# Eleven convolution taps go from TensorE to ScalarE products and GpSimd sums; VectorE's nine are all done in the projection

## The chip, the cores and the metric

The kernel runs on one core of one Trainium2 chip. The metric is the device time of one execution in microseconds, as the median of several runs. One execution was profiled; its trace and its page are what the numbers below are read from. PE is TensorE, DVE is VectorE, ACT is ScalarE, POOL is GpSimd, SP is SyncE, which here issues nearly all transfers.

## The reference

One step of a decoder layer for a prompt of 512 tokens and for 8 sample tokens. The part that matters here is the mixing sub-layer:

```python
z = rms_norm(x, norm_g) @ w_in                      # 1024 -> 2048 columns
gm_u, gm_v, cv_a, cv_b = jnp.split(z, [...], axis=-1)   # 512 each
u = jax.nn.gelu(gm_u)
v = layer_norm(jax.nn.gelu(gm_v), gm_ln_g, gm_ln_b)     # over each head's 128 channels
a_out = u * chunk_spatial_mix(v, gm_ws, gm_bs)
glu = cv_a * jax.nn.sigmoid(cv_b)
full = jnp.concatenate([conv_past, glu], axis=1)
conv = depthwise_conv(full, conv_w)  + conv_b           # 31 taps per channel, causal
b_out = jax.nn.silu(layer_norm(conv, cv_ln_g, cv_ln_b))
y = x + jnp.concatenate([a_out, b_out], axis=-1) @ w_out
```

After it come keys and values of 256 memory tokens, cross-attention with 4 heads, a mixture of 32 experts (one group of four, then two of its eight experts for each token) and a final norm. All is float32.

## The kernel before

Each engine has its own instruction list, and semaphores order the engines against each other. Nothing is scheduled by a tool: the order in the code is the order on the engine. Every engine waits in place, so what stands behind a waiting instruction waits too.

**Projection.** The product with w_in has 16 column blocks of 128 channels, m = 0 to 15, with the tokens along the free axis. Each float32 product is made of three passes (a high part and a low part of weights and activations, lines 1708 to 1710), 48 matmuls a block. For this ACT writes the high part w_h of a pair of blocks (split_h, line 739) and DVE the low part w_l (split_l, line 1057), one pair ahead. DVE takes each block out of PSUM and multiplies it by the token's norm rstd (line 1182). Blocks 0, 1, 4, 5 become the linear half of glu; blocks 2, 3, 6, 7 are its gates (ACT's sigmoid, then a DVE product that counts the semaphore glu_ready up); blocks 8 to 11 are v, and 12 to 15 are u (both by ACT's gelu, line 788). The norms rstd come out of a small chain: DVE writes five diagonal tiles, PE turns them into a row with all-ones matmuls (token_norms, line 1746), DVE copies the row (line 1118) and can only then empty the first blocks. token_norms stands behind block 2, and block 3 of PE needs the first block's PSUM back.

**Convolution.** glu has 4 groups of 128 channels, with 30 zero columns in front. A tap is a shifted copy of glu times one weight per channel. Of the 31 taps DVE does the first nine (V_TAPS) as `conv = glu * w + conv` (part_taps, lines 1148 and 1151), 36 instructions of 128x512: 28 of them between the blocks of the projection, by the table PART_AT, eight later. PE does the other 22 after the projection (conv_taps): per tap 16 matmuls of 32x512 with diagonal weights dw, each recorded as two, so 32 records a tap at line 1829. In front of the last tap PE adds DVE's part with one more group of 16 (line 1824), for which it waits for part_done. Between the taps stand four turnings of the memory tokens (mem_turned), which ACT and DVE empty.

**Around it.** After the projection DVE normalises v, 128 channels of 128 tokens at a time (line 1222), and POOL scales and shifts each tile by ln_g and ln_b (lines 2216 and 2218). PE needs v only behind the first block of memory keys. PE's next stage, the memory keys, follows the convolution directly; ACT empties the convolution's PSUM (line 820).

POOL does one mask and nothing else between its first 2 us and the normalisation of v. SP loads weight slots in one fixed order (STREAM); slots come free as split_l reads them.

Of the kernel before, what the change touches and what calls it, by code (L numbers as in the profile page):

```python
# [22 lines left out]
F32 = mybir.dt.float32  # L23
F32R = mybir.dt.float32r
I32 = mybir.dt.int32
ALU = mybir.AluOpType
# [3 lines left out]
P = 128  # L30
D = 1024
KT_D = D // P
SEQ = 512
NS = 8
# [9 lines left out]
PE_TAPS = TAPS - V_TAPS  # L44
# [117 lines left out]
def trunk_kernel(nc, a, outs):  # L162
# [6 lines left out]
    with ExitStack() as ctx:  # L169
# [93 lines left out]
        tail = at("tail", [PAST + NS, GM], F32, kT_at)  # L263
# [17 lines left out]
        mem_junk = at("mem_junk", [P, D], F32, kT_at + 4096)  # L281
# [130 lines left out]
        part_done = sem("part_done")  # L412
        conv_out = sem("conv_out")
# [7 lines left out]
        v_ready = sem("v_ready")  # L421
        v_scaled = sem("v_scaled")
# [4 lines left out]
        tail_stored = sem("tail_stored")  # L427
        gmv_stored = sem("gmv_stored")
# [18 lines left out]
        r_root = sem("r_root")  # L447
        x_stored = sem("x_stored")
        gk_in = sem("gk_in")
# [87 lines left out]
        def _(sp):  # L537
# [48 lines left out]
            for c in range(AT[("w_in", 1)], len(STREAM)):  # L586
# [12 lines left out]
                if c == 16:  # L599
                    sp.wait_ge(ta_used, TA_AT["tail"] + 1)  # L600
                    sp.dma_start(conv_prompt[0, 0], tail[0:PAST, :]).then_inc(tail_stored, 16)
                    sp.dma_start(conv_sample[0, :, PAST - 1, :], tail[PAST:PAST + NS, :]).then_inc(tail_stored, 16)
                if c == 16:
                    sp.wait_ge(v_ready, NT)
                    sp.dma_start(gmv_prompt[0, 0], v_tok[:, 3, :]).then_inc(gmv_stored, 16)
                    sp.dma_start(gmv_sample[0, :, 0, :], v_s[0:NS, :]).then_inc(gmv_stored, 16)
# [106 lines left out]
            sp.wait_ge(tail_stored, 32)  # L713
            sp.wait_ge(gmv_stored, 32)
# [6 lines left out]
        def _(act):  # L721
# [53 lines left out]

            for n in range(8):
# [51 lines left out]
            for n in range(8, 16):  # L828
                split_h(n + 1)
                if n == 9:  # L830
# [4 lines left out]
                    act.wait_ge(gmv_stored, 32)  # L835
# [114 lines left out]
            act.dma_start(gk[:], a["norm_ffn_g"][0].rearrange("(p k) -> p k", k=KT_D)).then_inc(gk_in, 16)  # L950
# [18 lines left out]
            act.activation(rs5[:], rs5[:], ACT.Sqrt).then_inc(r_root, 1)  # L969
# [34 lines left out]
            act.wait_ge(gk_in, 16)  # L1004
# [29 lines left out]
        def _(dve):  # L1034
# [86 lines left out]
            def tap_weights(i):  # L1121
# [5 lines left out]
                w = cols_b[:, V_TAPS:TAPS, i:i + 1].broadcast_to([P, PE_TAPS, BAND])  # L1127
# [36 lines left out]
            PART_AT = {4: 3, 5: 4, 6: 4, 7: 3, 8: 2, 9: 3, 10: 3, 11: 3, 14: 3}  # L1164
# [39 lines left out]
            dve.tensor_scalar(mv[:, :, :, 1], mv[:, :, :, 1], EPS, None, ALU.add).then_inc(v_mean, 1)  # L1204
            part_taps(2)
# [1162 lines left out]
```

## Time and profile before

| | |
|---|---|
| median of three runs | 686.86 us (686.58 to 687.76) |
| the profiled execution | 687.92 us, its span 686.0 us |
| TensorE busy | 595.5 us (87% of the span) |
| VectorE busy | 318.0 us (46%) |
| ScalarE busy | 197.9 us (29%) |
| GpSimd busy | 78.8 us (11%) |
| mean granted TensorE clock | 0.939 |
| HBM | 174.94 MB read, 15.61 MB written |

The span runs from the first to the last instruction; 1.9 us of the execution's own time lie around it. Shares of the span are averages over stages with different limits: the projection runs to 108.6 us, the convolution to 138.2, memory keys, output projection and attention to about 347, routing to 420, and the experts to 650.

### The profile page before, as it was taken

The page shows a single profiled execution, that of the slowest core. Times are in us where ns is not written, and L with a number is a line of the kernel's source. Part 1 is how long each engine was busy: PE and PEld are TensorE (multiplying, and loading weights), DVE is VectorE, ACT ScalarE, POOL GpSimd, SP SyncE. Part 2 cuts the span into 40 slices and gives each one's busy share as a digit, 9 for nine tenths or more (in the row PEclk, how much of TensorE's full clock was granted, in tenths as well). Part 3 has the DMA queues.
Part 4 walks back from the last instruction along what each step waited for, and adds up shares of the span by engine and source line. Part 5 has one row for each costly group of instructions (what it writes and reads, how often), then busy time and mean ns, then how long its engine had stood idle before and what let it go on. Part 6 is the DMA issues. An engine that isn't in the chain of part 4 may idle for free.

```text
span 686.0 us, 11980 instructions
## 1 busy us (share of the span) xinstructions
PE 595.5 (87%) x4915; PEld 467.8 (68%) x4915; DVE 318.0 (46%) x626; ACT 197.9 (29%) x337; POOL 78.8 (11%) x129
## 2 busy tenths in 40 slices
PE   5899999889999999999989966989989987489810
PEld 5899996567899999985788853555655664246400
DVE  4669787879644464788403174121121121011147
ACT  6422323154834344444012241111111111011132
POOL 0000000700002200010212101111111111110100
PEclk9999999999999999999989965999999999689965
DMA  8852210325544314679696396999999999999663
GB/s 328 315 222 103 83 63 3 125 83 180 188 149 168 123 63 134 250 305 419 233 392 262 131 406 231 364 421 418 420 417 421 419 421 420 419 420 415 259 266 127
DMA packets 35651, 181.56 MB, mean 265 GB/s; under 512 B 8943, under 2 KB 10127, under 8 KB 16765
## 3 DMA queue, kind: packets, MB, share of 16 engines
q1 hardware_dynamic: 26733, 165.62, 61.5%
q0 software_dynamic: 5600, 12.76, 4.9%
q10 hardware_dynamic: 3264, 2.42, 1.1%
q8 instruction: 39, 0.64, 0.4%
q14 instruction: 15, 0.12, 0.1%
HBM read 174.94 MB, written 15.61 MB: 278 GB/s over the span
## 4 chain that ended last, share of the span: by engine, by line
PE 68%; SPq 14%; DVE 7%; DMA 6%; issue 3%; ACT 2%; ACTq 0%; DVEq 0%; POOLq 0%
PE ps L1708 13%; PE ps L1710 13%; PE ps L1709 13%; SPq L626 9%; PE ps L2123 8%; PE ps L2151 4%; DMA w<-exp_w 4%; SPq L635 4%; PE ps L1829 4%; PE ps L1704 3%; PE ps L1909 2%; PE ps L1930 2%; PE ps L1971 1%; DVE x L1656 1%; DVE x L1658 1%
## 5 line engine op out<-in xcount | busy, mean ns | idle before, releaser
L1708 PE MATMUL ps<-xH,w_h 128*128 128x260 f32 x480 | 138.8, 289 | 2.3 <-DVE glu L1182 2.0
L1710 PE MATMUL ps<-xL,w_h 128*128 128x260 f32 x480 | 136.2, 284 | 0.0
L1709 PE MATMUL ps<-xH,w_l 128*128 128x260 f32 x480 | 136.2, 284 | 0.0
L2123 PE MATMUL ps<-w,xeT 128*64 128x256 f32 (+2 forms) x1024 | 120.7, 406 | 13.5 <-DMA w<-exp_w 12.2
L2123 PEld LDWEIGHTS ps<-w,xeT 128*64 128x64 f32 (+2 forms) x1024 | 81.8, 145 | 57.2 <-issue 29.4
L1708 PEld LDWEIGHTS ps<-xH,w_h 128*128 128x128 f32 x480 | 91.2, 190 | 6.3 <-issue 5.7
L1709 PEld LDWEIGHTS ps<-xH,w_l 128*128 128x128 f32 x480 | 91.2, 190 | 0.2
L1710 PEld LDWEIGHTS ps<-xL,w_h 128*128 128x128 f32 x480 | 91.1, 190 | 0.0
L1057 DVE TENSOR_TENSOR w_l<-raw,w_h 128x2048 fp32r<-128x2048 f32 x27 | 61.8, 2289 | 27.6 <-ACT w_h L739 27.4
L2151 PE MATMUL ps<-w,aT 128*64 128x512 f32 (+2 forms) x256 | 60.3, 627 | 16.1 <-DVE aT L1621 12.2
L739 ACT ACTIVATE w_h<-raw 128x2048 fp32r<-128x2048 f32 x27 | 51.6, 1910 | 21.9 <-PE ps L1710 19.2
L1614 DVE SCALAR_TENSOR_TENSOR gated<-ps,rs_slot,silu 128x256 f32<-128x256 f32 x14 | 6.8, 484 | 108.7 <-PE ps L2123 108.7
L2151 PEld LDWEIGHTS ps<-w,aT 128*64 128x64 f32 (+2 forms) x256 | 19.1, 140 | 46.4 <-issue 30.5
L987 ACT ACTIVATE xeT<-ps,gk 128x128 f32<-128x128 f32 x68 | 19.4, 368 | 86.8 <-PE ps L1704 86.8
L1628 DVE COPY ye<-ps 128x512 f32<-128x512 f32 x16 | 11.1, 692 | 64.5 <-PE ps L2151 64.5
L1710 PE MATMUL ps<-cL,w_h 128*128 128x260 f32 x128 | 36.2, 283 | 0.0
L1708 PE MATMUL ps<-cH,w_h 128*128 128x260 f32 x128 | 36.1, 282 | 0.0
L1709 PE MATMUL ps<-cH,w_l 128*128 128x260 f32 x128 | 36.0, 281 | 0.0
L2267 POOL DMA_INDIRECT y_rows<-ye,ids x14 | 14.1, 1008 | 172.3 <-DVE ye L1628 172.3
L1002 ACT ACTIVATE ye<-ps 128x512 f32<-128x512 f32 x16 | 9.6, 597 | 68.3 <-PE ps L2151 68.3
L1829 PE MATMUL ps<-glu,dw 32*32 32x512 f32 x704 | 26.9, 636 | 1.7 <-issue 1.7
L1352 DVE CUSTOM_DVE_ANT_0 ttr_out<-raw,qb 128x256 f32<-128x256 f32 x64 | 27.2, 424 | 2.4 <-DMA qb<-q_rows 0.4
(351 smaller groups left out, 859.5 us busy)
## 6 DMA issues: line engine op xcount, KB each, us to landing
w<-exp_w SPq DMA_DIRECT2D x96, 1024.0 KB, 22.9
raw<-weights SPq DMA_DIRECT2D x27, 1024.0 KB, 4.8
raw<-caches SPq DMA_DIRECT2D x16, 1024.0 KB, 7.8
qb<-q_rows POOLq DMA_DIRECT2D x4, 1024.0 KB, 5.6
yr<-y_rows SPq DMA_DIRECT2D x4, 1024.0 KB, 7.8
xT<-x_turned SPq DMA_DIRECT2D x4, 520.0 KB, 6.9
raw<-x_prompt SPq DMA_DIRECT2D x4, 512.0 KB, 12.0
x_rows<-x ACTq DMA_DIRECT2D x4, 512.0 KB
```

The lines of the kernel that those rows point to most:

```text
L626: sp.dma_start(dst[:, h:h + 1, :], src[bass.ds(e, 1)].rearrange("o p f -> p o f")).then_inc(w13_in[h][s], 16)
L635: sp.dma_start(w2s[s][:].rearrange("p k d -> p (k d)").rearrange("p (o f) -> p o f", o=1), w2[bass.ds(e, 1)].rearrange("o p f -> p o f")). ...
L739: act.activation(w_h[n % 2][:], slot[:], ACT.Copy).then_inc(h_ready, 1)
L1057: dve.tensor_tensor(w_l[n % 2][:], slot[:], w_h[n % 2][:].bitcast(F32), ALU.subtract).then_inc(l_ready, 1)
L1352: last = dve.tensor_tensor_reduce(ttr_out[:], keys[:, (2 * s4 + t) * XH_DIM:(2 * s4 + t + 1) * XH_DIM], qb[h % 2][:, s, :], 1.0, 0.0, ALU. ...
L1704: return pe.transpose(out, src, ident[0:n, 0:n])
L1708: pe.matmul(out, h1, h2, start=start, stop=False)
L1709: pe.matmul(out, l1, h2, start=False, stop=False)
L1710: return pe.matmul(out, h1, l2, start=False, stop=stop)
L1829: last = pe.matmul(out[r // 2][c * BAND:(c + 1) * BAND, r % 2, :], dw[c // 2][rows, c % 2, k - V_TAPS, :], glu[rows, c, k:k + SEQ], start= ...
L2123: last = pe.matmul((mm[0][half, j, 0:FF], ta[1][half, 0:FF])[h], xeT[j][:, k, half], w13[s][:, h, k, :], start=k == 0, stop=k == KT_D - 1)
L2151: last = pe.matmul(mm[1][half, b, :], aT[:, k, half], w2s[s][:, k, c], start=k == 0, stop=k == 1)
```

## The change

Eleven more taps, 9 to 19, leave PE. For each of them and each of the four channel groups ACT makes a product (a Copy activation of 128x512 with the tap's weights as scale), 44 in all; the first product of each group goes straight into tap_sum, the other 40 into two buffers in turn, from which POOL adds them to tap_sum. ACT's products stand in fours ahead of what it does for each of the blocks 4 to 14. ACT may write a buffer only when POOL has added what lay in it (product_added). PE keeps 11 taps, and adds conv and tap_sum ahead of the last of them, with 16 matmuls each.

DVE's nine taps are now all done by block 15. The normalisation of v is written as scalar_tensor_tensor, with the inverse deviation as a second tensor of stride zero, in place of tensor_scalar, and it is interleaved with the low parts of the memory tokens; the samples' row of v is scaled and shifted by DVE instead of POOL. token_norms moves from behind block 2 into it, ahead of its sixth of eight contraction steps. A few scratch tiles lie elsewhere, and some semaphores are merged.

```diff
-PE_TAPS = TAPS - V_TAPS
+POOL_TAPS = 11
+PE_FIRST = V_TAPS + POOL_TAPS
+PE_TAPS = TAPS - PE_FIRST
+PRODUCTS = [(k, c) for pair in ((0, 1), (2, 3)) for k in range(V_TAPS, PE_FIRST) for c in pair]
+PRODUCTS_AT = {m: 4 for m in range(4, 15)}
...
@@ scalar (ACT)
+            def products(count):
+                for _ in range(count):
+                    k, c = PRODUCTS[products_n[0]]
+                    products_n[0] += 1
+                    act.wait_ge(glu_ready, c + 1)
+                    if k == V_TAPS:
+                        dst = tap_sum[:, c, :]
+                    else:
+                        if sums_n[0] >= 2:
+                            act.wait_ge(product_added, sums_n[0] - 1)
+                        dst = product[sums_n[0] % 2][:]
+                        sums_n[0] += 1
+                    act.activation(dst, glu[:, c, k:k + SEQ], ACT.Copy, scale=cols_b[:, k, c:c + 1]).then_inc(product_made, 1)
...
                 for m in (2 * n, 2 * n + 1):
+                    products(PRODUCTS_AT.get(m, 0))
@@ vector (DVE)
-            PART_AT = {4: 3, 5: 4, 6: 4, 7: 3, 8: 2, 9: 3, 10: 3, 11: 3, 14: 3}
+            PART_AT = {4: 3, 5: 4, 6: 4, 7: 3, 8: 4, 9: 4, 10: 4, 11: 4, 14: 2, 15: 4}
...
+                    last = dve.scalar_tensor_tensor(row, row, mv[0:n_t, j, h, 0:1], mv[0:n_t, j, h, 1:2].broadcast_to([n_t, P]),
+                                                    ALU.subtract, ALU.mult)
...
-                    last = dve.tensor_scalar(row, row, mv[0:n_t, j, h, 0:1], mv[0:n_t, j, h, 1:2], ALU.subtract, ALU.mult)
@@ tensor (PE)
-                project("w_in", m, xH, xL)
-                if m == 2:
-                    pe.wait_ge(dve_made, 1)
-                    token_norms()
+                project("w_in", m, xH, xL, (lambda k: token_norms() if k == 5 else None) if m == 2 else None)
...
-            MEM_AT = {V_TAPS + 6: 2, V_TAPS + 8: 3}
+            MEM_AT = {PE_FIRST + 4: 2, PE_FIRST + 8: 3}
...
-                for k in range(V_TAPS, TAPS):
+                for k in range(PE_FIRST, TAPS):
...
                         pe.wait_ge(part_done, 4 * V_TAPS)
+                        pe.wait_ge(product_added, len(PRODUCTS) - 4)
+                        for part in (conv, tap_sum):
@@ gpsimd (POOL)
+            added, last_of = 0, {}
+            for i, (k, c) in enumerate(PRODUCTS):
+                if k == V_TAPS:
+                    continue
+                pool.wait_ge(product_made, i + 1)
+                if c in last_of:
+                    pool.wait_ge(product_added, last_of[c])
+                pool.tensor_tensor(tap_sum[:, c, :], tap_sum[:, c, :], product[added % 2][:], ALU.add).then_inc(product_added, 1)
+                added += 1
+                last_of[c] = added
```

On PE, in block 2 of the projection, the five rows of token_norms (tile diag) stood behind the block's last matmul:

```order
L1708 MATMUL ps<-xH,w_h_54 128x260
L1709 MATMUL ps<-xH,w_l_56 128x260
L1710 MATMUL ps<-xL,w_h_54 128x260
L1746 MATMUL ps<-diag,ones 128x128 x2
L1746 MATMUL ps<-diag,ones 128x4
L1746 MATMUL ps<-diag,ones 128x124
L1746 MATMUL ps<-diag,ones 128x128
L1746 MATMUL ps<-diag,ones 128x8
L1708 MATMUL ps<-xH,w_h_54 128x260
L1709 MATMUL ps<-xH,w_l_56 128x260
```

They are now 18 matmuls earlier, with three contraction steps of block 2 behind them; they are the same instructions.

On ACT, before, the work of blocks 8 to 10 was a high part (w_h), a table load and a gelu (out tile cHf) for each block:

```order
L739 ACTIVATE w_h_54<-raw_52 128x2048
L788 ACT_TABLE_LOAD
L788 ACTIVATE cHf<-zt_75 128x520
L788 ACTIVATE cHf<-zt_76 128x520
L739 ACTIVATE w_h_53<-raw_49 128x2048
L788 ACTIVATE cHf<-zt_75 128x520
```

In the same place of the changed kernel four products stand ahead of each gelu:

```order
L746 ACTIVATE w_h_54<-raw_52 128x2048
L798 ACTIVATE product_114<-glu,cols 128x512
L798 ACTIVATE product_115<-glu,cols 128x512
L798 ACTIVATE product_114<-glu,cols 128x512
L798 ACTIVATE product_115<-glu,cols 128x512
L813 ACT_TABLE_LOAD
L813 ACTIVATE cHf<-zt_75 128x520
L798 ACTIVATE product_114<-glu,cols 128x512
L798 ACTIVATE product_115<-glu,cols 128x512
L798 ACTIVATE tap_sum<-glu,cols 128x512 x2
L813 ACTIVATE cHf<-zt_76 128x520
L746 ACTIVATE w_h_53<-raw_49 128x2048
```

So the high part for the next pair of blocks (the last row) can start only when the products of both blocks ahead of it have found a free buffer.

## Rows read from the trace of the kernel before

**Rows 1.** The page, the chain that ended last, shares by engine.

```profile
PE 68%; SPq 14%; DVE 7%; DMA 6%; issue 3%; ACT 2%; ACTq 0%; DVEq 0%; POOLq 0%
```

**Rows 2.** Windows over the stages of the whole span.

```profile
core 0: us, PE busy (x) PEld busy (x) DVE busy (x) ACT busy (x) POOL busy (x), PEclk, DMA share, GB/s
...
42.00:108.60 66.60, 66.60 (x560) 66.30 (x558) 55.60 (x112) 16.70 (x17) 0.00 (x0) 1.00 0.25 87
108.60:138.20 29.60, 27.88 (x745) 15.96 (x744) 22.57 (x40) 7.68 (x17) 12.85 (x10) 0.94 0.20 74
...
520.00:650.00 130.00, 107.25 (x796) 65.68 (x794) 18.49 (x34) 17.92 (x49) 17.01 (x20) 0.93 0.98 402
```

**Rows 3.** The chain that ended last, 100 to 160 us: start, us, what.

```profile
118.66 9.62 PE ps L1829 x258
128.28 1.72 issue
...
138.14 1.27 ACT cLf L820 x2
```

**Rows 4.** Line 1829 alone in three windows.

```profile
120.36:126.63 6.27, 6.27 (x218) 4.37 (x203) 1.00 0.59 220
130.06:134.88 4.82, 4.82 (x104) 2.78 (x109) 0.65 0.01 3
108.60:138.20 29.60, 26.77 (x704) 14.40 (x704) 0.94 0.20 74
```

**Rows 5.** PE's timeline at the end of block 2.

```profile
26.71 1.59 PE L1746 MATMUL ps<-diag,ones 128*128 128x128 f32 x12
30.25 0.36 PE L1708 MATMUL ps<-xH,w_h 128*128 128x260 f32 x1 [1.95 <-DVE glu L1182]
```

**Rows 6.** DVE's timeline around the token norms.

```profile
22.77 1.00 DVE L1115 TENSOR_SCALAR diag<-ident,tok_ss 128x128 f32<-128x128 f32 x5
27.48 0.43 DVE L1118 COPY rstd<-ps 128x260 f32<-128x260 f32 x1 [3.70 <-PE ps L1746]
```

**Rows 7.** Groups by line on ACT, 34 to 109 us.

```profile
L739 ACT ACTIVATE w_h<-raw 128x2048 fp32r<-128x2048 f32 x6 | 11.4, 1903 | 8.4 <-PE ps L1710 8.4
L788 ACT ACTIVATE cHf<-zt 128x520 f32<-128x520 f32 x4 | 2.6, 640 | 15.9 <-DVE zt L1182 15.9
```

**Rows 8.** Groups by line on DVE, 0 to 150 us.

```profile
L1151 DVE SCALAR_TENSOR_TENSOR cLf<-glu,cols,cLf 128x512 f32<-128x512 f32 x32 | 22.3, 745 | 0.0
L1057 DVE TENSOR_TENSOR w_l<-raw,w_h 128x2048 fp32r<-128x2048 f32 x9 | 20.6, 2287 | 3.7 <-ACT w_h L739 3.6
...
L1160 DVE TENSOR_TENSOR glu<-glu,zt 128x520 f32<-128x520 f32 x4 | 2.8, 690 | 0.0
L1135 DVE TENSOR_TENSOR conv_s<-conv_s,cols 128x248 f32<-128x248 f32 x4 | 2.5, 618 | 0.1
```

**Rows 9.** The second gate on DVE and the last weights' high part on ACT.

```profile
42.62 0.69 DVE L1160 TENSOR_TENSOR glu<-glu,zt 128x520 f32<-128x520 f32 x1
...
96.34 1.90 ACT L739 ACTIVATE w_h<-raw 128x2048 fp32r<-128x2048 f32 x1
```

**Rows 10.** POOL's timeline, the first two of its instructions on v.

```profile
121.93 1.30 POOL L2216 TENSOR_TENSOR v_tok<-v_tok,ln_g 128x512 f32<-128x512 f32 x1 [88.70 <-DVE v_tok L1222]
123.32 1.28 POOL L2218 TENSOR_TENSOR v_tok<-v_tok,ln_b 128x512 f32<-128x512 f32 x1
```

**Rows 11.** Line 1222, durations in ns (min/median/max).

```profile
L1222 DVE TENSOR_SCALAR v_tok<-v_tok,mv x16: 333/341/1436, 120.7 to 130.8; 128x128 f32<-128x128 f32 x16
```

**Rows 12.** One place where VectorE and GpSimd overlap, 242.4 to 243.6 us.

```profile
242.51 0.76 DVE L1086 SCALAR_TENSOR_TENSOR xL<-xT,cols,xH 128x520 fp32r<-128x520 f32 x1
...
243.08 1.38 POOL L2210 TENSOR_TENSOR sumsq<-sumsq,zt 128x520 f32<-128x520 f32 x1 [4.15 <-ACT zt L745]
```

**Rows 13.** Durations of those two lines, 200 to 246 us.

```profile
L1086 DVE SCALAR_TENSOR_TENSOR xL<-xT,cols,xH x8: 749/750/760, 207.2 to 242.5; 128x520 fp32r<-128x520 f32 x8
L2210 POOL TENSOR_TENSOR sumsq<-sumsq,zt x7: 1302/1330/1377, 208.6 to 243.1; 128x520 f32<-128x520 f32 x7
```

More of the change, by code:

```diff
@@ L262, in trunk_kernel @@
         xs_rows = at("xs_rows", [NS, D], F32, cl_at)
-        tail = at("tail", [PAST + NS, GM], F32, kT_at)
+        tail = at("tail", [P // 2 + PAST + NS, GM], F32, s_at)[P // 2:]
+        tap_sum = at("tap_sum", [P, 4, SEQ], F32, kT_at)
+        product = [at(f"product{i}", [P, SEQ], F32, v_at + 2 * PE_TAPS * BAND * 4 + 4 * SEQ * i) for i in range(2)]
         v_raw = cHf[:, 0:4, :]
@@ L968, in _ @@
             act.wait_ge(tv_used, TV_AT["r2"] + 1)
-            act.activation(rs5[:], rs5[:], ACT.Sqrt).then_inc(r_root, 1)
+            act.activation(rs5[:], rs5[:], ACT.Sqrt).then_inc(rs_root, 1)
             for j, (t0, n) in enumerate(TILES):
@@ L1820, in conv_taps @@
                         pe.wait_ge(part_done, 4 * V_TAPS)
-                        for r in range(4):
-                            rows = slice(r * BAND, (r + 1) * BAND)
-                            for c in range(4):
-                                pe.matmul(out[r // 2][c * BAND:(c + 1) * BAND, r % 2, :], ident[rows, rows],
-                                          conv[rows, c, 0:SEQ], start=False, stop=False)
+                        pe.wait_ge(product_added, len(PRODUCTS) - 4)
+                        for part in (conv, tap_sum):
+                            for r in range(4):
+                                rows = slice(r * BAND, (r + 1) * BAND)
+                                for c in range(4):
+                                    pe.matmul(out[r // 2][c * BAND:(c + 1) * BAND, r % 2, :], ident[rows, rows],
+                                              part[rows, c, 0:SEQ], start=False, stop=False)
                     for r in range(4):
@@ L1828, in conv_taps @@
                         for c in range(4):
-                            last = pe.matmul(out[r // 2][c * BAND:(c + 1) * BAND, r % 2, :], dw[c // 2][rows, c % 2, k - V_TAPS, :],
-                                             glu[rows, c, k:k + SEQ], start=k == V_TAPS, stop=k == TAPS - 1)
+                            last = pe.matmul(out[r // 2][c * BAND:(c + 1) * BAND, r % 2, :], dw[c // 2][rows, c % 2, k - PE_FIRST, :],
+                                             glu[rows, c, k:k + SEQ], start=k == PE_FIRST, stop=k == TAPS - 1)
                         if k == TAPS - 1 and r % 2:
```

82 lines of the change are left out of this document (49 added, 33 removed).

## Prediction

> **What bounds the kernel now.** I first read the chain that ended last [rows 1]: 68% of it is PE, the rest mostly the weight transfers of the experts. The windows by stage [rows 2] say where. In the projection (42.0 to 108.6 us) PE is busy for all of its 66.6 us, DVE for 55.6, ACT for 16.7 and POOL for none. In the convolution (108.6 to 138.2) PE is busy for 27.9 of 29.6 us. What is taken from PE in either stage moves the end, as long as the engines that feed it keep pace. The last stages are paced by transfers (DMA share 0.98 from 520 to 650), but every load in them is released by work before it, and between 42 and 138 us the transfers are at 0.20 to 0.25. So a shift in the convolution should reach the end whole.
>
> The chain inside the convolution [rows 3] is line 1829 up to ACT's emptying of PSUM at 138.14, with one hole: from 128.28 PE waits 1.72 us for nothing that the profile shows. Behind the hole the granted clock falls: 1.00 in the window from 120.36, 0.65 in the one from 130.06, 0.94 over the stage [rows 4].
>
> **The change, part by part.**
>
> *Taps off PE.* The window from 120.36 to 126.63 holds six taps (192 of its 218 records start there, the others are under way at its edges): 1.045 us a tap [rows 4]. The bound above is the stage's whole busy time over its 22 taps, 26.77/22 = 1.22, which has the slow stretch in it. Eleven taps go and one group of 16 matmuls for tap_sum comes, of a tap's shape and so at a tap's price: ten fewer, 10.45 us (up to 12.2). The four memory turnings stay.
>
> *The hole and the low clock.* In the window from 130.06 three taps took 4.82 us, 1.7 more than at 1.045. If hole and slow stretch don't come back, up to 3.4 us more are gained. Nothing in the diff addresses them; I take zero, and the 3.4 into the range.
>
> *token_norms.* Its matmuls end at 28.3 and block 3 starts at 30.25, after 1.95 us of waiting for DVE [rows 5]. The diagonals are ready at 23.8 [rows 6]; block 2 ends at 26.7. Nine blocks lie between the two rows of [rows 9], 5.9 us each, so one of a block's eight contraction steps is 0.73 and the new place, three steps ahead, is at about 24.5. DVE's copies then start about 2.2 us earlier and end with the evictions before block 2's own end. Gain: the 1.95 us.
>
> *DVE.* Eight of its 36 tap instructions move ahead of the end of the projection, at 0.70 us each (22.3 us over 32) [rows 8]: 5.6 us, and half of the weights' building goes. It has 66.6 - 55.6 = 11 us free there [rows 2], and less to do afterwards. Cost on the path: nothing, if its durations hold.
>
> *ACT.* 44 products of 128x512. A 128x520 activation takes 0.64 us [rows 7]: 28 us on top of 16.7, in 66.6. In program order they stand ahead of gelus and of high parts, so what counts is not their length but their wait for a free buffer: ACT can be at most two adds ahead of POOL.
>
> *POOL.* 40 additions of 128x512. The same form takes 1.30 us and is followed 0.09 us later by the next that waits for it (121.93 to 123.32) [rows 10]: 1.39 each, 55.6 us. The first can start after the second gate (43.3), the last ends at about 99, well ahead of the last tap.
> The tight place is the high part of the last weights, on ACT at 96.34 [rows 9]. In the changed kernel 32 products stand ahead of it, so 28 additions must be done. From 43.3 to 96.3 that allows 53/28 = 1.89 us an addition. At 1.39 there is slack of 0.5.
>
> *The price that the trace lacks:* how long a two-input DVE instruction and a POOL addition take side by side. From 42 to 108.6 us POOL is idle before. Bounds: below, nothing is added. Above, line 1222: its 16 instructions, 0.34 us in the median, take up to 1.44 when an addition of POOL is running [rows 11], that is, they stand still until it has ended, while POOL's 1.30 stays. If the taps and low parts behave so, the two engines take turns. In the 53 us window POOL's 28 additions are 36.4 us, DVE's 30 taps 21.0, four low parts 9.2, two gates and four products for the samples 3.9 [rows 8]: 70.5 us, 17.5 more than there are.
> Which end? The nearest row is the one place where a two-input form of each overlaps, at 243.08 [rows 12]: DVE's took 760 ns where the other seven took 749 or so, POOL's 1377 where the median is 1330 [rows 13]. Nobody stood still, but the overlap is 0.19 us, DVE came first, and both were the longest of their kind, by 10 and 47 ns. I take +0.05 us an addition, which the slack of 0.5 covers. This is the weakest step.
> The Trainium skill speaks against it (SBUF — State Buffer, "Who interferes with whom"): an instruction of VectorE with two SBUF inputs takes the read interface that it shares with GpSimd, against a GpSimd instruction that reads SBUF, and whoever comes second stands still until the first is done. By its rule the form of the normalisation doesn't matter either, since the new one has two SBUF inputs as well. What that would make of the sum is the second case below.
>
> *After the projection.* DVE's way to the memory's deviation and v's to PE ended on DVE with line 1222, whose 16 instructions took from 120.7 to 130.8 and more [rows 11], with eight taps ahead of them, while PE's convolution took 29.6. Now PE's takes 19, and DVE's, without the 5.6 us of taps and with 16 instructions at some 0.34, about 12. Only if the normalisation still waits for POOL's additions (some 1.2 us for each of eight) does DVE's become the longer one, by up to 6 us.
>
> **The sum**, against the profiled execution's own 687.92 us (span 686.0 and 1.9 around it): 687.9 - 10.45 - 1.95 = 675.5. The median of the runs is 1.1 lower than that execution, so the sum lies at 674.4 on the median's scale; for small waits at buffers I say 675.
>
> **The ways in which it could go.**
> *1. PE's relief arrives (0.52).* 675, its own range 670 (dearer taps, hole and slow clock gone) to 678.
> *2. DVE and POOL take turns (0.36).* Mechanism: POOL's additions slow to (36.4 + 34.1)/28 = 2.5 us, ACT's products wait for buffers, the next weights' high part stands behind them, and PE waits in blocks 8 to 14. It costs 17.5 us of PE's time in the projection against 12.4 gained: 687.9 + 5 = 693; with up to 6 us at the normalisation 699. Slower, about 696 (688 to 704). It decides from 1.89 + 12.4/28 = 2.33 us an addition. For it: rows 11, and both durations of rows 13 being the longest. Against it: line 1222 is a one-tensor form, and no two-input instruction stood still.
> *3. The two slow each other in part (0.08).* Additions of 2.0 to 2.2 us: a PE loss of 3 to 9 us, 679 to 686. Faster still.
> *4. The gain is eaten further on (0.04).* If the experts' loads started when they start now, the 0.98 share from 520 on [rows 2] would hold the end: 687. Against it: they are released by counters of the stages before, and at a share of 0.20 to 0.25 in the changed stages no transfer is behind.
>
> **How the numbers follow.** The likeliest case gives 675. Cases of both signs hold most of the chance, so the range goes from 671 to 699: it leaves out the upper third of case 2 and the edges of case 1. A run of this kernel can tell about 0.2% (1.4 us) from no change. Faster 0.60 (cases 1 and 3), the same 0.04, slower 0.36.
>
> **What would show it.** In the changed kernel's profile: line 1871 (taps) with 352 records in place of 704, and a convolution stage of 16 to 19 us; no wait before block 3; POOL's additions at a start-to-start of 1.4 us and DVE's taps still at 745 ns. Wrong would be: taps or low parts of 1.3 us or more, additions 2 us or more apart, holes in PE between blocks 8 and 14 with ACT's products waiting for POOL, or a granted clock below 1.00 in the projection because of such holes.

## The result and the profile after

The changed kernel takes 703.5 us (median of 4 runs, 701.3 to 704.7), the kernel before beside it 686.8 (686.6 to 687.8). The ratio is 1.0231, with a 95% interval of 1.0205 to 1.0257: slower, above the range. The profiled execution took 702.4 us with a span of 700.5.

The page, the chain that ended last, which answers to [rows 1]:

```profile
PE 56%; DVE 15%; SPq 14%; issue 6%; DMA 6%; ACT 2%; ACTq 0%; DVEq 0%; POOLq 0%
```

DVE has come into the chain (7% to 15%). The windows over the stages, the first with the bounds that the projection had before [rows 2], the next four from stage to stage as they now lie (rest of the projection, convolution, hole behind it, memory keys up to the channel sums):

```profile
core 0: us, PE busy (x) PEld busy (x) DVE busy (x) ACT busy (x) POOL busy (x), PEclk, DMA share, GB/s
42.00:108.60 66.60, 55.38 (x431) 54.34 (x429) 65.33 (x60) 36.63 (x47) 55.62 (x32) 0.95 0.20 71
108.60:128.50 19.90, 15.50 (x107) 15.01 (x108) 17.01 (x52) 8.84 (x12) 14.73 (x9) 0.83 0.16 54
128.50:144.80 16.30, 16.02 (x432) 8.92 (x433) 14.85 (x28) 7.46 (x15) 6.87 (x6) 1.00 0.07 11
144.80:152.50 7.70, 1.00 (x58) 0.35 (x32) 6.35 (x13) 1.38 (x4) 3.43 (x3) 0.80 0.62 257
152.50:165.50 13.00, 12.12 (x61) 9.94 (x61) 8.84 (x15) 6.35 (x6) 0.00 (x0) 0.86 0.35 108
```

The projection, in which PE had no free time before, now lasts to 128.5 us in place of 107.5. PE is idle for 11 of the first 66.6 us, and DVE is the busy engine: 65.3 of 66.6, where it had 55.6. From 42.0 to 128.5 us PE is busy for 70.9 of 86.5 us, with six waits that add up to the other 15.6. What ended them (us in total, times, longest):

```profile
PE ps L1750 <- DVE zt L1208: 6.5, 3, 2.9
PE ps L1746 <- DVE stats L1223: 6.0, 2, 5.2
PE ps L1746 <- ACT cHf L813: 3.1, 1, 3.1
```

So PE waits for DVE to empty PSUM (12.5 us) and for one gelu of ACT (3.1), and not for the high or low part of the weights. And PE's own work became slower: the granted clock is 0.50 from 67.5 to 70.9, 84.6 to 88.0 and 111.9 to 118.7 us. The convolution is short, as intended: 16.3 us from the projection's end to its last matmul, where the same stretch of the kernel before shows 30.2:

```profile
107.50:137.70 30.20, 28.48 (x754) 16.89 (x753) 23.34 (x41) 7.66 (x16) 12.85 (x10) 0.94 0.19 73
139.60:150.80 11.20, 10.40 (x60) 8.58 (x60) 8.79 (x15) 6.30 (x6) 0.00 (x0) 1.00 0.39 121
```

Behind it stands a hole of nearly 7 us that the kernel before had not. From stage to stage, by the starts and ends of PE's records, the span changed by +21.0 (projection), -13.9 (convolution), +5.8 (its end to the first matmul of the memory's keys: 1.9 to 7.7 us), +1.8 (keys up to the channel sums: 11.2 to 13.0 us, at a granted clock of 0.86 in place of 1.00) and -0.2 for all that follows: +14.5.

Groups by line on POOL, DVE and ACT of the changed kernel, for [rows 8] and [rows 10]:

```profile
L2263 POOL TENSOR_TENSOR tap_sum<-tap_sum,product 128x512 f32<-128x512 f32 x40 | 70.3, 1792 | 20.6 <-ACT product L798 20.6
L1176 DVE SCALAR_TENSOR_TENSOR cLf<-glu,cols,cLf 128x512 f32<-128x512 f32 x32 | 40.0, 1303 | 0.0
L798 ACT ACTIVATE product<-glu,cols 128x512 f32<-128x512 f32 x40 | 28.1, 718 | 25.9 <-POOL tap_sum L2263 25.9
```

and their durations one by one (min/median/max in ns), with two lines that read PSUM:

```profile
L2263 POOL TENSOR_TENSOR tap_sum<-tap_sum,product x40: 1272/1712/3685, 43.3 to 124.2; 128x512 f32<-128x512 f32 x40
L1176 DVE SCALAR_TENSOR_TENSOR cLf<-glu,cols,cLf x32: 735/1547/1846, 43.4 to 131.4; 128x512 f32<-128x512 f32 x32
L1208 DVE TENSOR_TENSOR zt<-ps,rstd x12: 684/688/701, 30.4 to 128.8; 128x520 f32<-128x520 f32 x12
L1223 DVE BATCH_NORM_STATS2 stats<-ps x20: 269/280/288, 111.2 to 124.4; 128x6 f32<-128x128 f32 x16, 8x6 f32<-8x128 f32 x4
```

This is the picture of two engines that take turns. A tap alone takes 745 ns [rows 8]; here half of them take twice that. An addition alone takes 1.30 us; here it takes 1.79 in the mean and up to 3.69. From the start of the first to the start of the last the 40 additions are 2.08 us apart in the mean, with POOL's waits for products (20.6 us) in it. Lines 1208 and 1223, whose input comes from PSUM, kept their time. The longest addition can be read in single rows, DVE first, then POOL (four additions in one row), then ACT:

```profile
68.42 2.06 DVE L1176 SCALAR_TENSOR_TENSOR cLf<-glu,cols,cLf 128x512 f32<-128x512 f32 x3
70.41 2.28 DVE L1082 TENSOR_TENSOR w_l<-raw,w_h 128x2048 fp32r<-128x2048 f32 x1
...
73.22 1.17 DVE L1185 TENSOR_TENSOR glu<-glu,zt 128x520 f32<-128x520 f32 x1
74.32 1.26 DVE L1159 COPY conv_s<-glu 128x8 f32<-128x8 f32 x1
...
70.15 8.28 POOL L2263 TENSOR_TENSOR tap_sum<-tap_sum,product 128x512 f32<-128x512 f32 x4 [2.65 <-ACT product L798]
...
73.93 0.72 ACT L798 ACTIVATE product<-glu,cols 128x512 f32<-128x512 f32 x1 [3.24 <-POOL tap_sum L2263]
```

The first addition (70.15, 3.69 us) begins while the last of three taps is running (until 70.48). The low part follows that tap at once, and the addition ends at 73.84, 1.15 us after the low part has ended at 72.69: it stood still behind both. By the recorded starts it came 0.26 us before the low part, so these starts don't tell who goes first. ACT waits 3.24 us for its buffer. The copy of 128x8 elements at 74.32 takes 1.26 us, nearly all of it standing still behind an addition.

And the end of the convolution: PE's timeline, then the chain that ended last over the same stretch.

```profile
145.37 0.44 PE L1879 MATMUL ps<-cs,ident 128*32 128x8 f32 x32
152.55 0.77 PE L1750 MATMUL ps<-w_h,xH 128*128 128x512 f32 x1 [6.74 <-ACTq L850]
```

```profile
140.98 5.13 DVE v_tok L1247 x7
...
146.90 2.57 DVE v_s L1247 x4
149.50 0.69 DVE v_s L1264
...
150.21 0.68 DVE v_s L1265
150.89 0.09 DVE m_ss L1269
151.00 0.20 ACT m_ss L836
151.20 1.16 ACT cLf L845 x2
...
152.55 0.77 PE ps L1750
```

PE waits for the PSUM buffers of the convolution. ACT empties them at line 845, but in its program the square root of m_ss (line 836) stands ahead of that; it waits for DVE's line 1269, and this one stands behind the normalisation, which POOL's scaling of v holds up. Lines 1264 and 1265, 1.4 us in the same chain, are the scaling and shifting of the samples' row that the change took from POOL to DVE.

### The profile page after: what moved, and what is told of

Same layout as the page of the kernel before. It is cut to its first block, busy times and chain, and to the rows that moved or that the text cites. A ratio compares the mean times of both kernels' runs of the same rounds, so it can differ in the third digit from the quotient of the medians.

```text
span 700.5 us, 11500 instructions
## 1 busy us (share of the span) xinstructions
PE 592.7 (85%) x4595; PEld 467.3 (67%) x4595; DVE 344.5 (49%) x628; ACT 227.3 (32%) x381; POOL 146.6 (21%) x167
## 4 chain that ended last, share of the span: by engine, by line
PE 56%; DVE 15%; SPq 14%; issue 6%; DMA 6%; ACT 2%; ACTq 0%; DVEq 0%; POOLq 0%
PE ps L1750 11%; PE ps L1752 10%; PE ps L1751 10%; SPq L634 8%; PE ps L2166 8%; PE ps L2194 4%; DMA w<-exp_w 4%; SPq L643 4%; DVE cLf L1176 2%; PE ps L1746 2%; PE ps L1952 2%; PE ps L1973 2%; DVE v_tok L1247 1%; DVE w_l L1082 1%; PE ps L2014 1%
## 5 line engine op out<-in xcount | busy, mean ns | idle before, releaser
L1750 PE MATMUL ps<-xH,w_h 128*128 128x260 f32 x480 | 141.4, 295 | 6.8 <-DVE zt L1208 6.5
L1752 PE MATMUL ps<-xL,w_h 128*128 128x260 f32 x480 | 138.5, 289 | 0.0
L1751 PE MATMUL ps<-xH,w_l 128*128 128x260 f32 x480 | 138.4, 288 | 0.0
L1750 PEld LDWEIGHTS ps<-xH,w_h 128*128 128x128 f32 x480 | 93.7, 195 | 11.4 <-issue 9.3
L1751 PEld LDWEIGHTS ps<-xH,w_l 128*128 128x128 f32 x480 | 93.6, 195 | 0.2
L1752 PEld LDWEIGHTS ps<-xL,w_h 128*128 128x128 f32 x480 | 93.5, 195 | 0.0
L1082 DVE TENSOR_TENSOR w_l<-raw,w_h 128x2048 fp32r<-128x2048 f32 x27 | 64.5, 2391 | 27.7 <-ACT w_h L746 27.6
L2263 POOL TENSOR_TENSOR tap_sum<-tap_sum,product 128x512 f32<-128x512 f32 x40 | 70.3, 1792 | 20.6 <-ACT product L798 20.6
L2194 PEld LDWEIGHTS ps<-w,aT 128*64 128x64 f32 (+2 forms) x256 | 19.1, 140 | 46.0 <-issue 30.2
L1176 DVE SCALAR_TENSOR_TENSOR cLf<-glu,cols,cLf 128x512 f32<-128x512 f32 x32 | 40.0, 1303 | 0.0
L798 ACT ACTIVATE product<-glu,cols 128x512 f32<-128x512 f32 x40 | 28.1, 718 | 25.9 <-POOL tap_sum L2263 25.9
```

Source lines behind the costliest of these rows:

```text
L798: act.activation(dst, glu[:, c, k:k + SEQ], ACT.Copy, scale=cols_b[:, k, c:c + 1]).then_inc(product_made, 1)
L1082: dve.tensor_tensor(w_l[n % 2][:], slot[:], w_h[n % 2][:].bitcast(F32), ALU.subtract).then_inc(l_ready, 1)
L1176: ins = dve.scalar_tensor_tensor(conv[:, c, 0:SEQ], src, w, conv[:, c, 0:SEQ], ALU.mult, ALU.add)
L1750: pe.matmul(out, h1, h2, start=start, stop=False)
L1751: pe.matmul(out, l1, h2, start=False, stop=False)
L1752: return pe.matmul(out, h1, l2, start=False, stop=stop)
```

## The experiments

Five experiments ask about the additions, one about the norms, one about the number of additions, and the others about the hole behind the convolution. The lines of the kernels differ by one or two from those of the changed kernel; the tiles' names tell them apart.

**No additions.** In the changed kernel POOL only counts; the taps' sum is left out of the output.

```diff
-pool.tensor_tensor(tap_sum[:, c, :], tap_sum[:, c, :], product[added % 2][:], ALU.add).then_inc(product_added, 1)
+pool.sem_inc(product_added, 1)
```

> The changed kernel without POOL's 40 additions (ACT's products are made and not summed, so these taps' sum is left out; POOL only counts them). Theory A (a VectorE instruction with two SBUF inputs and a POOL instruction that reads SBUF can't run side by side): DVE's 32 tap instructions are back at 745 ns, no holes in PE's projection, and 673 to 677 us, the 675 of the first case. Rival B (ACT's 44 products in front of gelus and high parts, or DVE's fuller list, are what delays PE): 690 us or more, with the holes still there.

Measured: 679.3 us (678.7 to 682.6), ratio to before 0.9897 [0.986, 0.9934]. The projection ends at 105.6 us: before's 107.5 less the norms' 1.9. So ACT's 44 products, DVE's eight more taps and their order cost PE nothing, and the additions alone cost it 128.5 - 105.6 = 22.9 us. The taps are back at their own time:

```profile
L1176 DVE SCALAR_TENSOR_TENSOR cLf<-glu,cols,cLf x32: 741/746/753, 43.2 to 108.5; 128x512 f32<-128x512 f32 x32
```

But the hole stays without them, and the low clock behind it is even longer. The windows are convolution, hole, and keys up to the channel sums:

```profile
105.60:121.90 16.30, 16.01 (x432) 8.92 (x433) 14.85 (x28) 7.47 (x15) 6.86 (x6) 1.00 0.04 8
121.90:129.60 7.70, 1.00 (x58) 0.35 (x32) 6.35 (x13) 1.38 (x4) 3.43 (x3) 0.69 0.64 264
129.60:143.40 13.80, 12.92 (x61) 10.53 (x61) 8.87 (x15) 6.36 (x6) 0.00 (x0) 0.80 0.31 102
```

There are two losses, then, and this one belongs to the rest of the change.

**POOL busy, but only writing.** Each addition replaced by four memsets of a scratch tile, in a chain; the taps' sum is left out here too.

```diff
-pool.tensor_tensor(tap_sum[:, c, :], tap_sum[:, c, :], product[added % 2][:], ALU.add).then_inc(product_added, 1)
+for z in range(4):
+    if 4 * added + z:
+        pool.wait_ge(product_added, 4 * added + z)
+    pool.memset(scratch[:], 0.0).then_inc(product_added, 1)
```

> The changed kernel with each addition of POOL replaced by a chain of four memsets of 128x256 into unused memory, each waiting for the one before, about 1.3 to 1.6 us together, which read nothing (the sum of the eleven taps is left out). Theory A, in its narrow form (only POOL instructions that read SBUF hold a VectorE instruction with two SBUF inputs): DVE's taps at 745 ns, no holes in the projection, and the 679 of the run without additions, within 3 us. Rival C (ACT's wait for a slow POOL with two buffers delays PE, or whatever POOL does beside DVE costs it): taps over 1.0 us or holes in PE, 686 us or more.

Measured: 681.1 us (680.4 to 681.6), ratio 0.9897 [0.9856, 0.9939]. POOL is as busy as 40 undisturbed additions would have made it, ACT waits 20.6 us for its buffers, and DVE's taps notice nothing:

```profile
L2265 POOL MEMSET scratch<- 128x256 f32 x160 | 50.5, 316 | 26.0 <-ACT product L799 15.2
L1177 DVE SCALAR_TENSOR_TENSOR cLf<-glu,cols,cLf x32: 733/746/751, 43.6 to 111.8; 128x512 f32<-128x512 f32 x32
```

The projection ends at 108.8, 3.2 us later than without any work on POOL. So POOL's being busy and ACT's waits for it explain at most 3.2 of the 22.9 us. What is left between memsets and additions is that the additions read SBUF.

**One input in place of two.** POOL copies each product to tap_sum.

```diff
-pool.tensor_tensor(tap_sum[:, c, :], tap_sum[:, c, :], product[added % 2][:], ALU.add).then_inc(product_added, 1)
+pool.tensor_copy(tap_sum[:, c, :], product[added % 2][:]).then_inc(product_added, 1)
```

> The changed kernel with POOL's 40 additions replaced by 40 copies of the product to tap_sum (one SBUF input in place of two; the sum of the taps is left out). A POOL copy of 128x520 takes 0.62 us in the profile of before, an addition 1.30. Theory (any POOL instruction that reads SBUF and a VectorE instruction with two SBUF inputs take turns): VectorE's taps of the projection show single values up to 745 + 620 = 1.36 us and a mean above 0.85, POOL's copies a mean above 0.7; the sum of work is 28 x 0.62 + 34.1 = 51.4 us for 53, so PE loses little, 679 to 683. Rival (only a POOL instruction with two inputs takes turns): taps stay at 745 ns and copies at 0.62, and the time is that without additions, 679.3 within 0.5.

Measured: 679.1 us (678.8 to 681.1), ratio 0.9886 [0.9847, 0.9924]. The groups by line (busy, mean):

```profile
L2263 POOL COPY tap_sum<-product 128x512 f32<-128x512 f32 x40 | 39.9, 1018 | 28.6 <-ACT product L798 28.4
L1176 DVE SCALAR_TENSOR_TENSOR cLf<-glu,cols,cLf 128x512 f32<-128x512 f32 x32 | 26.0, 868 | 0.0
```

and one by one (min/median/max):

```profile
L2263 POOL COPY tap_sum<-product x40: 609/620/3405, 42.9 to 102.1; 128x512 f32<-128x512 f32 x40
L1176 DVE SCALAR_TENSOR_TENSOR cLf<-glu,cols,cLf x32: 740/746/1178, 43.1 to 109.3; 128x512 f32<-128x512 f32 x32
```

By the rows one input is enough: 400 ns a copy and 122 ns a tap are lost in the mean, and a copy of 0.62 us took up to 3.41. In time it costs next to nothing: the projection ends at 106.4, 0.8 us later than without any work on POOL. That the sum of both engines' work fits here is the likely reason; it was not tested by itself.

**More buffers.** Four product buffers in place of two, so ACT may be four products ahead. Two of them lie where ACT's squares of the memory tokens are written later, so those wait for the last addition.

```diff
-if sums_n[0] >= 2:
-    act.wait_ge(product_added, sums_n[0] - 1)
-dst = product[sums_n[0] % 2][:]
+if sums_n[0] >= 4:
+    act.wait_ge(product_added, sums_n[0] - 3)
+dst = product[sums_n[0] % 4][:]
```

> The changed kernel with four product buffers in place of two (ACT may be four additions ahead of POOL). Theory A: DVE's and POOL's instructions still take turns, DVE's taps stay near 1.3 us and the additions near 1.8; ACT waits less, but PE waits for DVE's evictions and low parts; 1 to 5 us less, 698 to 702. Rival D (two buffers are too few, ACT's 25.9 us of waits for POOL are what PE loses): 690 us or less.

Measured: 701.3 us (701.0 to 702.1), ratio 1.0208 [1.0176, 1.0241]. ACT's wait for buffers fell from 25.9 to 5.9 us, and the projection ended at 127.1 in place of 128.5. PE still waits there for DVE's emptying (7.6 us for line 1209, 4.5 for line 1224) and 3.2 us for ACT's gelu. So the waits for buffers are not the path to PE. What is short is the two engines' common time, which no buffer adds to.

**The form of the normalisation.** Back to the one-tensor form, all else as changed.

```diff
-last = dve.scalar_tensor_tensor(row, row, mv[0:n_t, j, h, 0:1], mv[0:n_t, j, h, 1:2].broadcast_to([n_t, P]),
-                                ALU.subtract, ALU.mult)
+last = dve.tensor_scalar(row, row, mv[0:n_t, j, h, 0:1], mv[0:n_t, j, h, 1:2], ALU.subtract, ALU.mult)
```

> The changed kernel with the normalisation back in the form with two per-partition numbers (tensor_scalar), all else as changed. Theory A: either form is held by POOL's additions for their whole length, so no difference: within 1 us of the changed kernel's 702 to 704. Rival F (the two-tensor form is held less, as the change's title may mean): 3 us or more slower than the changed kernel.

Measured: 701.5 us (701.1 to 704.2), ratio 1.0211 [1.0166, 1.0256]: the same as with the two-tensor form. First row this kernel, then the changed one:

```profile
L1247 DVE TENSOR_SCALAR v_tok<-v_tok,mv x16: 333/340/1448, 134.3 to 144.6; 128x128 f32<-128x128 f32 x16
```

```profile
L1247 DVE SCALAR_TENSOR_TENSOR v_tok<-v_tok,mv x16: 338/347/1443, 135.2 to 145.8; 128x128 f32<-128x128 f32 x16
```

Both forms stand still behind POOL for up to 1.44 us, as line 1222 did in [rows 11].

**The norms alone.** The kernel before, with token_norms moved to the contraction step that the change gives it.

```diff
-project("w_in", m, xH, xL)
-if m == 2:
-    pe.wait_ge(dve_made, 1)
-    token_norms()
+project("w_in", m, xH, xL, (lambda k: token_norms() if k == 5 else None) if m == 2 else None)
```

> The kernel before with token_norms moved ahead of the sixth contraction step of block 2, nothing else. By the prediction's term: the wait of 1.95 us before block 3 goes and nothing else changes, 684.9 us (ratio 0.997). If block 3 then waits for the next thing (weights, DVE's emptying): less than 1 us gained.

Measured: 685.4 us (683.0 to 691.1, 12 runs), ratio 0.9973 [0.9951, 0.9996]; the projection ends at 105.9, 1.6 us earlier than before.

**Five taps in place of eleven.** 16 additions, two a block; 17 taps stay on PE. Scratch tiles lie elsewhere, to make room.

```diff
-POOL_TAPS = 11
+POOL_TAPS = 5
-PRODUCTS_AT = {m: 4 for m in range(4, 15)}
+PRODUCTS_AT = {m: 2 for m in range(4, 14)}
```

> The changed kernel with five taps in place of eleven as products on ScalarE and sums on POOL (16 additions in place of 40, two a block from 4 to 13), so 17 taps on PE. Theory (the engines take turns, and PE loses only what their sum of work is over the time there is): 16 additions x 1.30 + VectorE's 34.1 us = 54.9 us of work for the 53 us up to the last weights, so about 2 us of loss, 4.2 us of taps and 1.95 of norms gained, and a hole behind the longer convolution of 1 to 2 us: 682 to 684, faster than before. Rival (each addition costs PE its share of the 21 us, whatever their number): 16/40 x 21 = 8.4 us lost in the projection, 688 to 690.

Measured: 685.8 us, ratio 0.9967 [0.9941, 0.9994], faster than before by a hair. The projection ends at 110.8: 5.2 us lost, between the two expectations (2 and 8.4), the taps at 924 ns in the mean. Together: no additions 105.6, 16 additions 110.8, 40 additions 128.5. The first 16 cost 0.33 us each, the other 24 cost 0.74 each. The cost of an addition grows with their number, but the first ones are not free: from 42.0 to 110.8 us PE stands idle for 3.2 us, behind DVE's batch statistics and ACT's gelu, and is busy for 2.0 us more than without additions, with 3.4 us at a granted clock of 0.50 in it. Five taps give 4.2 us by the price of a tap, 5.7 by the length of the convolution, and cost 5.2.

**v's scale and shift later.** The changed kernel, with POOL starting on v only when DVE has normalised all four tiles.

```diff
-pool.wait_ge(v_norm, j + 1)
+pool.wait_ge(v_norm, NT - 1)
```

> The changed kernel, only that POOL starts to scale and shift v when DVE has normalised all four tiles. Theory A: the 16 instructions of the normalisation fall from 706 ns to about 340, DVE reaches the memory's deviation some 5 to 6 us earlier, the hole of 6.9 us behind the convolution shrinks to 1 to 2 us, and the half clock behind it may go: 695 to 698 us. Rival E (ACT or PE wait there for something else than DVE's normalisation, such as the low parts of the memory or the transfers): the hole stays above 5 us, 701 us or more.

Measured: 703.5 us (702.6 to 705.3), ratio 1.0223 [1.018, 1.0266]. The hole was not shortened. The four tiles are now undisturbed, and the samples' rows, which come next on DVE, take their place:

```profile
L1247 DVE SCALAR_TENSOR_TENSOR v_tok<-v_tok,mv x16: 345/347/353, 134.9 to 139.6; 128x128 f32<-128x128 f32 x16
L1247 DVE SCALAR_TENSOR_TENSOR v_s<-v_s,mv x4: 1337/1392/1418, 141.4 to 145.4; 8x128 f32<-8x128 f32 x4
```

The waits moved from 128-row tiles to 8-row ones, which stand still as long, and m_ss came at 151.5, as late as ever.

**The convolution emptied first.** The changed kernel, additions and all, with ACT's square root of m_ss moved behind its emptying of the convolution.

```diff
-act.wait_ge(m_mean, 1)
-act.activation(m_ss[:], m_ss[:], ACT.Sqrt).then_inc(m_root, 1)
 for r in range(4):
     ...
+act.wait_ge(m_mean, 1)
+act.activation(m_ss[:], m_ss[:], ACT.Sqrt).then_inc(m_root, 1)
```

> The changed kernel with two instructions in another order on ScalarE: the emptying of the convolution's PSUM now stands ahead of the square root of m_ss, which waits for VectorE. Everything else, the additions too, as changed. Theory (ScalarE stands at m_ss behind VectorE's slow normalisation, and PE behind the PSUM buffer): the hole of 6.9 us behind the convolution shrinks to about 2.5 us, where the low parts of the memory (ready at 147.3, convolution's end at 144.8) and the emptying itself (2.7 us) are next; 703.5 - 4.5 = 699, and down to 696 if the low clock behind the hole goes too. Rival (PE waits there for v or for the memory's low parts, and m_ss only ends last by chance): the hole stays above 5 us and the time at 702 to 703.5.

Measured: 698.0 us (697.8 to 698.5), ratio 1.015 [1.0113, 1.0187]; 5.5 us less than the changed kernel. ACT's timeline:

```profile
144.52 2.66 ACT L842 ACTIVATE cLf<-ps,cols 128x512 f32<-128x512 f32 x4 [2.25 <-PE ps L1870]
150.24 0.20 ACT L850 ACTIVATE m_ss<-m_ss 128x2 f32<-128x2 f32 x1 [3.06 <-DVE m_ss L1268]
```

The emptying no longer waits. From the convolution's last matmul to the keys' first it is now 2.1 us in place of 7.7, and the keys run at full clock. m_ss comes at 150.2, 0.8 us before the changed kernel's, and now PE's keys don't wait for it. A new wait of 2.4 us in the mixing of v (for vsT, until 155.8), with 3.4 us at a granted clock of 0.50 right behind it, gives some back.

**Twelve taps on DVE, none on POOL.** The kernel before with the norms moved and three more taps on DVE, once with v's scale and shift on POOL held back until the normalisation is through (first), once without that and with the convolution emptied first (second).

```diff
-V_TAPS = 9
+V_TAPS = 12
-PART_AT = {4: 3, 5: 4, 6: 4, 7: 3, 8: 2, 9: 3, 10: 3, 11: 3, 14: 3}
+PART_AT = {4: 3, 5: 4, 6: 4, 7: 3, 8: 4, 9: 4, 10: 4, 11: 4, 14: 2, 15: 4}
```

> A version that theory A suggests, from the kernel before: no products on ACT and no additions on POOL; token_norms moved; DVE takes twelve taps in place of nine (36 of its 48 instructions in the projection, 12 behind it), and POOL starts on v when DVE has normalised all of it. PE loses three taps of 1.045 us and the wait of 1.4 to 1.95 us: 681 to 683 us (ratio 0.992 to 0.994). If DVE's fuller list makes PE wait in the projection or behind the convolution: 685 us or more.

> The kernel before with the norms moved ahead as changed, twelve taps on VectorE in place of nine (in the blocks where the changed kernel has them, and six more behind), no products and no additions, POOL's scale and shift of v as before, and the convolution's PSUM emptied ahead of m_ss's square root. Theory: 19 taps on PE in place of 22 give 3 x 1.045 = 3.1 us, the norms 1.95; VectorE's normalisation is slowed by POOL's eight additions as before, but nothing of PE waits for it, since v is ready at some 133 and is wanted at some 137: 686.8 - 5.1 = 681.7 (680 to 683). Rival (three more taps on VectorE bring the wait for v of 5.9 us that the run with twelve taps and the later scale of v had, whatever the order): 686 to 688.

Measured: 687.9 us (686.0 to 689.3), ratio 0.9999 [0.9979, 1.002] for the first, and 683.5 (682.0 to 685.4), 0.994 [0.9919, 0.9961] for the second. The first shows once more what POOL does to its neighbour, here behind the convolution (DVE, then POOL):

```profile
135.81 3.38 DVE L1057 TENSOR_TENSOR w_l<-raw,w_h 128x2048 fp32r<-128x2048 f32 x1
...
133.03 2.29 POOL L2216 TENSOR_TENSOR v_tok<-v_tok,ln_b 128x512 f32<-128x512 f32 x1
...
137.11 3.19 POOL L2216 TENSOR_TENSOR v_tok<-v_tok,ln_b 128x512 f32<-128x512 f32 x1
```

v's last rows came at 142.9, PE waited 5.5 us for them, and the 5 us gained before were gone. (The scaling of v began only at 126.5 there, because it was held back.) In the second v was ready at 138.6 and PE's wait for v_s was 0.9 us, with another of 2.0 for vsT behind it. The two versions differ in two edits at once, so these runs don't tell the shares of the two.

**v on DVE alone.** The second of these, and DVE scales and shifts v itself, so that no two instructions meet.

```diff
-last = dve.tensor_scalar(row, row, mv[0:n_t, j, h, 0:1], mv[0:n_t, j, h, 1:2], ALU.subtract, ALU.mult)
+last = dve.scalar_tensor_tensor(row, row, mv[0:n_t, j, h, 0:1], ln_g[0:n_t, at_h], ALU.subtract, ALU.mult)
+...
+last = dve.scalar_tensor_tensor(row, row, mv[0:n_t, j, h, 1:2], ln_b[0:n_t, at_h], ALU.mult, ALU.add)
```

> The last kernel with twelve taps on VectorE, norms moved ahead and the convolution's PSUM emptied ahead of m_ss, and now VectorE scales and shifts v itself, in the two-tensor form (two instructions of 128x128 a head in place of one, 40 in place of 20), so that POOL has no addition beside VectorE there. Theory (it is the turns with POOL that make v late, at 138.6 us, and PE wait for it): 40 x 0.27 = 10.7 us of VectorE from 121.2, v ready at about 132.5, no wait of PE for v (2.3 us) and no low clock behind it (up to 1.7): 683.5 - 3 = 680.5 (679 to 682). Rival (20 more instructions on VectorE make the weights' low part or the groups of the convolution late instead, which costs as much as the turns did): 683 to 685.

Measured: 682.3 us (680.0 to 685.1, 6 runs), ratio 0.9923 [0.9895, 0.9952]: the fastest version that leaves nothing out, 0.8% under the kernel before. Against the step before it (683.5) the gain is not resolved by the totals, but the mechanism is by the rows. The normalisation's first instructions one by one, then the timeline of DVE and PE behind the convolution:

```profile
L1222 DVE SCALAR_TENSOR_TENSOR v_tok<-v_tok,mv,ln_g x16: 346/347/351, 121.2 to 128.6; 128x128 f32<-128x128 f32 x16
```

```profile
136.24 2.29 DVE L1056 TENSOR_TENSOR w_l<-raw,w_h 128x2048 fp32r<-128x2048 f32 x1
...
132.51 0.47 PE L1713 MATMUL ps<-w_h,xH 128*128 128x512 f32 x1 [0.40 <-ACTq L822]
```

DVE does POOL's ten passes in 20 more short instructions: all 40 take 11.2 us, where the 20 of the normalisation alone, undisturbed, took 5.2 in the first version with twelve taps. It is done with v at 132.4: earlier than the 138.6 that it took with POOL's help. PE's low clock behind the convolution is gone.

## Why the prediction was wrong

**What failed first: "The price that the trace lacks".** The step took +0.05 us an addition, from the one place where two-input forms of both engines overlapped [rows 12, 13]. Measured it is +0.49 us an addition (1.79 for 1.30) and +0.56 a tap (1.30 for 0.745). The other end of that step, that they take turns, is what happens: not the busy POOL (memsets leave the taps at 746 ns), not the buffers (four gain 1.4 us of 22.9), not the form of the normalisation. The Trainium skill states this (SBUF — State Buffer, "Who interferes with whom"): a VectorE instruction with two SBUF inputs and a GpSimd instruction that reads SBUF exclude each other, and the later one stands still. The trace agrees, and adds what it amounts to: a wait for what is left of the other's instruction, up to 2.4 us for an addition behind a tap and a low part, 1.1 us for a copy of 8 columns (1.26 us, where the shortest of its kind took 0.16). What misled was an overlap of 0.19 us with DVE first: under this rule it can cost POOL 0.19 us at most, and the row was 0.05 above its median. It could not tell the theories apart; rows 11, an addition long enough to stand in the way, could.

Of the prediction's two arguments against turns, the second was this row; the first was that line 1222 is a one-tensor form. Back in that form it stood still as the two-tensor form did (1.45 and 1.44 us at most), so this was no argument either.

**The second case had the mechanism, and its size partly by luck.** It took its deadline from the wrong row. The high part at 96.34 [rows 9] belongs to the memory keys, whose first matmul comes at 139.6. The last weights of the projection, those with 32 products ahead of them in ACT's program, are the high part before that one. In the kernel before, then in the changed one:

```profile
84.39 1.90 ACT L739 ACTIVATE w_h<-raw 128x2048 fp32r<-128x2048 f32 x1
```

```profile
100.70 1.92 ACT L746 ACTIVATE w_h<-raw 128x2048 fp32r<-128x2048 f32 x1
```

From 43.3 to 84.39 there are 1.47 us for each of 28 additions, not 1.89, so that the first case's slack was 0.08 and not 0.5 if nothing may be late; PE reached the block that needs these weights at 95.6. The path was another one too. By the prediction's own scale (its third case, additions of 2.0 to 2.2 us) additions 2.08 us apart cost PE 3 to 9 us, by way of ACT's buffers and the high part. They cost 22.9, and by way of DVE's own program: the slow taps stand ahead of DVE's emptying of the next block, and PE waits for that. 15.6 us of the 22.9 are waits of PE, 12.5 of them ended by DVE, and 7.3 are slower work (busy for 70.9 us, where the run without additions has 63.6 in the same work). Most of that falls into the three stretches at a granted clock of 0.50, which the prediction had as a sign and not as a cost. That 70.5 - 53 = 17.5 comes near the 22.9 is likely because DVE, busy for 65.3 of 66.6 us, was indeed what ran out; no run tells that from chance.

The whole sum with what was measured: 687.9 - 1.9 (norms) + 22.9 (additions) - 13.9 (convolution) + 5.8 (hole) + 1.8 (keys) - 0.2 = 702.4, the profiled execution.

**The taps off PE** were right. The sum had 10.45 us; the stage gave 13.9, because the hole of 1.72 us "issue" and the low clock of [rows 3, 4] did not come back, which the range had at up to 3.4. It comes out the same, within 0.2 us, in every version with 11 taps (16.3 us). **token_norms** gave 1.6 to 1.9 of the 1.95. **ACT and DVE's own work** cost nothing, as the step said: without the additions PE is busy through all of the projection.

**"After the projection" was the second failure.** It let DVE's way to the memory's deviation become the longer one "only if the normalisation still waits for POOL's additions", and priced DVE otherwise at 12 us against PE's 19. The condition was true, as it had been before: the normalisation waited for POOL's own scaling of v, in the kernel before, in the changed one and in the run without additions. The time was under-read: from the projection's end DVE took 22.5 us to m_ss, and PE's convolution 16.3. By estimate some 7 of the 22.5 are waits behind POOL: 16 instructions at 706 ns in place of 347, four of the samples at 712 in place of 328 or so. The rest, about 15, is still more than the 12 of the step, which named neither the samples' rows nor their scaling, but less than PE's 16.3. Hence a hole in which PE waits for 6.7 us, and the low clock behind it (in the run without additions 0.80 in the mean up to the channel sums, for which PE took 2.6 us longer). That is why the run without additions gave 679.3 and not 675 or less: 675.5 - 3.4 (more from the convolution) + 5.8 + 2.6 = 680.5. The first case's 675 was thus out of reach even without the main fault. The place of the wait is shown by the emptying moved ahead: the hole went, and the convolution and DVE's normalisation were unchanged.

**What stays open.** Why PE's granted clock stays at 0.50 for 6.8 us in the changed kernel and for 10.2 in the run without additions, both with a wait of 6.7 us behind the convolution, is not explained by these runs. Nor is it which of the two engines goes first when both want to start: the recorded starts don't decide it. The stall of 1.7 us "issue" in a long convolution is open as well; it is there with 17, 19 and 22 taps on PE (0.7 to 1.7 us) and absent with 11. Eleven taps with no sharing at all, on an engine that doesn't collide, was not tried, since none has the time.

## What to carry to other kernels

Before work is given to an idle GpSimd, look at what VectorE does in the same stretch. If both read SBUF, and VectorE's forms are of the kind that wait, add their busy times together; the sum has to fit. Where it only just fits, single waits already reach the engine that sets the end (16 additions cost 5.2 us). Then follow the program of the engine that is slowed, and not only of the one that hands over the buffers: what stands behind the slow instructions there comes late. The same work as more instructions on VectorE may be cheaper than on an idle neighbour, as it was for v here: 6 us more of VectorE, and v was ready some 6 us earlier.

To price an overlap, use a row in which the second instruction comes well before the first has ended. A small excess over a short overlap says nothing.

When a stage on the bounding engine is made shorter, list what the other engines must finish by its end and look for an instruction in their program that waits for something not needed yet. Here one square root ahead of four evictions cost 5.5 us, where the shorter convolution had gained 13.9.

## What the runs showed of the hardware

- A VectorE tap of 128x512 (745 ns alone) took up to 1.85 us beside GpSimd's additions, an addition (1.30 alone) up to 3.69: it waited for the rest of a tap and for the 2.28 us instruction that followed the tap at once. The one that waits is charged with the whole wait in its own duration; nothing shows in the table of waits.
- A small instruction waits as long as a large one: a VectorE copy of 128x8 took 1.26 us, an 8x128 normalisation 1.39 in place of 0.33, and a one-tensor instruction on 128x2 numbers 1.21 in place of 0.15 (with v's scaling held back).
- One-tensor forms and copies of VectorE from SBUF to SBUF stand still as two-tensor forms do. Forms that read PSUM (688 ns for 128x520) and the batch statistics (280 ns) don't, and the additions beside them ran at 1.28 to 1.31 us.
- GpSimd's memsets don't disturb VectorE's taps (160 memsets, taps at 746 ns), but VectorE's four copies of 128x8 took 0.20 to 0.35 us beside them in place of 0.17, and each ended 0.03 to 0.04 us after the memset that was running. GpSimd's copies with one SBUF input disturb the taps (868 ns in the mean, up to 1.18 us).
- A VectorE reduction of 128x248 from SBUF (0.41 us) kept its time beside an addition.
